# Decay products in 64-row tiles and skip coefficients per chunk of tokens, in a two-layer hybrid encoder

## What is computed

```python
def ssd_scan(xdt, a, bm, cm):
    ...
    a_cum = jnp.cumsum(a, axis=-1)
    lmat = jnp.exp(segsum(a))                 # exp(a_cum[i] - a_cum[j]) for i >= j, else 0
    cb = jnp.einsum("bclgn,bcsgn->bcgls", Cc, Bc)
    y_diag = jnp.einsum("bcgls,bgecls,bcsgep->bclgep", cb, lmat, X)
    ...
    y_off = jnp.einsum("bclgn,bcgepn,bgecl->bclgep", Cc, states_in, jnp.exp(a_cum))
    return (y_diag + y_off).reshape(b, s, h, p)
...
    y_f = ssd_scan(X * dt[:, :, 0, :, None], dt[:, :, 0] * A[0], bm, cm)
    flip = lambda t: jnp.flip(t, axis=1)
    y_b = flip(ssd_scan(flip(X * dt[:, :, 1, :, None]), flip(dt[:, :, 1] * A[1]), flip(bm), flip(cm)))
    y = y_f + y_b + X * d_skip[:, None]
```

## Time and profile before

| | |
|---|---|
| median of 3 executions | 1734.44 us |
| lowest, highest | 1731.61, 1737.55 us |
| the profiled execution | 1734.82 us |
| its span | 1733.1 us |
| TensorE busy | 1676.0 us (97%) |
| VectorE, ScalarE, GpSimd busy | 692.6, 636.9, 658.0 us |
| mean DMA rate | 307 GB/s |

### The profile page before, as it was taken

How to read it: one execution, slowest core, us unless ns; L and a number is a source line. 1 busy time by engine, 2 the same in 40 slices (tenths; PEclk the granted TensorE clock), 3 DMA queues, 4 the chain that set the end, 5 groups by cost and what they waited for, 6 DMA issues and landing times.

```text
span 1733.1 us, 22654 instructions
## 1 busy us (share of the span) xinstructions
PE 1676.0 (97%) x8727; PEld 1043.4 (60%) x8727; DVE 692.6 (40%) x1367; ACT 636.9 (37%) x1327; POOL 658.0 (38%) x532
## 2 busy tenths in 40 slices
PE   8999999999999999898999999999999999999998
PEld 6889777787434444343378897777864434444343
DVE  6738875524112212121176388745241212222122
ACT  5565566754111111111156555667441111111111
POOL 7888777894000000000077987778930000000000
PEclk9999999999999999999999999999999999999999
DMA  7554313758999999999954452227689999999997
GB/s 277 213 193 156 149 59 134 286 229 327 386 411 426 427 428 428 427 428 426 412 219 162 179 202 104 106 107 300 235 329 395 422 428 427 428 428 427 427 425 297
DMA packets 54193, 531.72 MB, mean 307 GB/s; under 512 B 7464, under 2 KB 11784, under 8 KB 23600
## 3 DMA queue, kind: packets, MB, share of 16 engines
q1 hardware_dynamic: 54048, 530.17, 74.8%
q0 software_dynamic: 32, 0.02, 0.0%
HBM read 528.71 MB, written 2.42 MB: 306 GB/s over the span
## 4 chain that ended last, share of the span: by engine, by line
PE 77%; DMA 11%; SPq 6%; ACT 2%; DVE 2%; issue 1%; POOL 1%; DVEq 0%; ACTq 0%
PE PS L1344 18%; DMA view<-in_w_exp_down_dram 11%; PE PS L1372 9%; PE PS L928 9%; PE PS L930 9%; PE PS L929 9%; SPq L699 5%; PE PS L1034 3%; PE PS L1035 3%; PE PS L1036 3%; PE PS L1284 2%; PE PS L1129 2%; PE PS L1270 1%; PE PS L1074 1%; PE PS L916 1%
## 5 line engine op out<-in xcount | busy, mean ns | idle before, releaser
L2414 POOL TENSOR_TENSOR view<-view,view 128x512 fp32r<-128x512 f32 x448 | 576.6, 1309 | 550.9 <-ACT view L1504 540.0
L1344 PE MATMUL PS<-view,view 128*64 128x512 f32 x2044 | 456.3, 598 | 20.8 <-issue 20.0
L1504 ACT ACTIVATE view<-view 128x512 fp32r<-128x512 f32 x448 | 273.7, 629 | 153.9 <-PE PS L930 150.4
L1344 PEld LDWEIGHTS PS<-view,view 128*64 128x64 f32 x2044 | 152.4, 137 | 294.9 <-issue 291.5
L928 PE MATMUL PS<-view,view 128*128 128x512 f32 x704 | 286.9, 407 | 5.4 <-POOL view L2414 3.5
L930 PE MATMUL PS<-view,view 128*128 128x512 f32 x704 | 276.2, 392 | 0.0
L929 PE MATMUL PS<-view,view 128*128 128x512 f32 x704 | 276.1, 392 | 0.0
L1372 PE MATMUL PS<-view,stb 128*64 128x512 f32 x1024 | 230.4, 597 | 8.2 <-DMA view<-in_w_exp_down_dram 5.4
L2321 DVE SCALAR_TENSOR_TENSOR view<-PS,gcol,view 128x512 fp32r<-128x512 f32 x64 | 48.1, 751 | 446.6 <-ACT view L1808 446.5
L928 PEld LDWEIGHTS PS<-view,view 128*128 128x128 f32 x704 | 133.1, 189 | 33.6 <-issue 6.1
L1372 PEld LDWEIGHTS PS<-view,stb 128*64 128x64 f32 x1024 | 71.7, 136 | 131.9 <-issue 115.2
(11 more groups left out here) (260 smaller groups left out, 1875.9 us busy)
## 6 DMA issues: line engine op xcount, KB each, us to landing
view<-in_w_exp_up_dram SPq DMA_DIRECT2D x56, 2048.0 KB, 27.3
view<-in_w_exp_down_dram SPq DMA_DIRECT2D x56, 2048.0 KB, 29.2
view<-in_w_mix_dram SPq DMA_DIRECT2D x54, 2048.0 KB, 7.6
view<-in_w_exp_gate_dram SPq DMA_DIRECT2D x52, 2048.0 KB, 30.3
view<-in_w_exp_gate_dram SPq DMA_DIRECT2D x20, 512.0 KB, 30.7
view<-in_w_exp_down_dram SPq DMA_DIRECT2D x20, 512.0 KB, 13.5
view<-in_w_exp_gate_dram SPq DMA_DIRECT2D x8, 1024.0 KB, 6.6
view<-in_w_exp_up_dram SPq DMA_DIRECT2D x8, 1024.0 KB, 8.7
```

Of the source, the lines that this page charges most:

```text
L1344: ins = pe.matmul(bank(ph, name, j)[e * CAP:(e + 1) * CAP, :], xgT1[:, k, at + e * CAP:at + (e + 1) * CAP], rows, start=(k == 0), stop=(k ...
L1504: nc.scalar.activation(highs(chunk), weights(slot8, chunk), ACT.Copy).then_inc(*high_ready.up(ph))
L2414: g_.tensor_tensor(weights(low8, chunk), weights(slot8, chunk), highs(chunk), ALU.subtract).then_inc(*low_ready.up(ph))
```

## The change

Two edits. The rows of direction 1 in the tile `terms` go from 32 to 64, and the decay products read 33 rows at 0 and 33 at 64; the 18 rows behind the 15 of the terms hold the frame's zeros. ROWS goes from 47 to 97, and with it the frame and each read of a tile.

The skip coefficients of chunk 0 are made in step 0 and those of chunk 1 in step 2, each behind that step's mask product, with the addition of d_skip for each chunk by itself. `decays` counts three instead of two, and GpSimd waits for its chunk's coefficients at each of its products with them.

```diff
--- before.py
+++ after.py
@@ -81,7 +81,8 @@
 UNITS_SCAN = TT * SSM_GROUPS
 SPLIT, FOUR = 3, 4
 TERMS = SPLIT * FOUR + SPLIT
-ROWS = 32 + TERMS
+HALF_ROWS, USED = 64, 33
+ROWS = HALF_ROWS + USED
 TERM_WORDS = (P + FOUR * P) // 2
 TERM_RING = 3
 FEED = (("v1", FB, -1, 5), ("ga", FB + 1, 5, 10), ("gm", FB + 2, 10, ATT))
@@ -123,8 +124,8 @@
     for d in range(2):
         for part in range(SPLIT):
             for n in range(FOUR):
-                frame[32 * d + part * FOUR + n, P + n * P:P + (n + 1) * P] = one
-            frame[32 * d + SPLIT * FOUR + part, 0:P] = one
+                frame[HALF_ROWS * d + part * FOUR + n, P + n * P:P + (n + 1) * P] = one
+            frame[HALF_ROWS * d + SPLIT * FOUR + part, 0:P] = one
     return np.ascontiguousarray(frame).view(np.float32)


@@ -522,7 +523,7 @@
         terms_out = sig("terms_out", 4 * SPLIT * TT, 0, step=16)
         terms_in = [sig(f"terms_in{k}", len(range(k, ATT, TERM_RING)), 0, step=16) for k in range(TERM_RING)]
         chosen = sig("chosen", ATT, 0)
-        decays = sig("decays", 2, 0)
+        decays = sig("decays", 1 + TT, 0)
         nmx_ready = sig("nmx_ready", ATT, 0)
         p_ready = sig("p_ready", ATT, 0)
         at_ready = sig("at_ready", ATT, 0)
@@ -712,7 +713,7 @@
                         for part, d, c in product(range(SPLIT), range(2), range(TT)):
                             src = rows_out[kind][part * SSM_HEADS:(part + 1) * SSM_HEADS].rearrange(
                                 "h (c d l) -> h c d l", c=TT, d=2)[:, c, d, :]
-                            row = 32 * d + (SPLIT * FOUR + part if kind else part * FOUR)
+                            row = HALF_ROWS * d + (SPLIT * FOUR + part if kind else part * FOUR)
                             at = (c * (ATT // TT) * ROWS + row) * TERM_WORDS + (P // 2 if kind else 0)
                             to = [[TERM_WORDS * ROWS, ATT // TT], [P // 2 if kind else TERM_WORDS, FOUR], [1, P // 2]]
                             sp.dma_start(bass.AP(terms_dram.tensor, at, to), src).then_inc(*terms_out.up(ph))
@@ -1059,7 +1060,7 @@
                     else:
                         pe.wait_ge(*M_ready.at(ph, i))
                     for d in range(2):
-                        t_ = terms[i % TERM_RING][32 * d:32 * d + TERMS, :].bitcast(BF16)
+                        t_ = terms[i % TERM_RING][HALF_ROWS * d:HALF_ROWS * d + USED, :].bitcast(BF16)
                         ins = pe.matmul(PS[:, 4 + d, :], t_[:, 0:P], t_[:, P:], start=True, stop=True)
                     ins.then_inc(*fill(ph, "D", j, q))

@@ -2104,19 +2105,17 @@
                         v.tensor_tensor(M[:, 4 * q:4 * q + 4, :], PS[:, 5, :].rearrange("p (h l) -> p h l", h=4),
                                         cbt[:, j, :].unsqueeze(1).to_broadcast([P, 4, P]), ALU.mult
                                         ).then_inc(*M_ready.up(ph))
-                    if i == 0:
-
-                        dve.wait_ge(*out_of(ph, "cb", 1))
-                        for c_ in range(TT):
-                            link(v.tensor_tensor(M[:, 4:8, :], cbt[:, c_ * SSM_GROUPS:(c_ + 1) * SSM_GROUPS, :],
-                                                 ident[:, :].unsqueeze(1).to_broadcast([P, SSM_GROUPS, P]), ALU.mult))
-                            link(v.tensor_reduce(cb_diag[:, c_, :], M[:, 4:8, :], AX, ALU.add))
-                        for c_ in range(TT):
-                            link(v.tensor_tensor(coef[:, c_, :].rearrange("p (g e) -> p g e", g=SSM_GROUPS),
-                                                 dtv[:, c_, SSM_HEADS:].rearrange("p (g e) -> p g e", g=SSM_GROUPS),
-                                                 cb_diag[:, c_, :].unsqueeze(2).to_broadcast([P, SSM_GROUPS, GH]), ALU.mult))
-                        v.tensor_tensor(coef, coef, bc_d.unsqueeze(1).to_broadcast([P, TT, SSM_HEADS]), ALU.add
-                                        ).then_inc(*decays.up(ph))
+                    if i in (0, 2):
+
+                        c_ = i // 2
+                        dve.wait_ge(*out_of(ph, "cb", c_))
+                        link(v.tensor_tensor(M[:, 4:8, :], cbt[:, c_ * SSM_GROUPS:(c_ + 1) * SSM_GROUPS, :],
+                                             ident[:, :].unsqueeze(1).to_broadcast([P, SSM_GROUPS, P]), ALU.mult))
+                        link(v.tensor_reduce(cb_diag[:, c_, :], M[:, 4:8, :], AX, ALU.add))
+                        link(v.tensor_tensor(coef[:, c_, :].rearrange("p (g e) -> p g e", g=SSM_GROUPS),
+                                             dtv[:, c_, SSM_HEADS:].rearrange("p (g e) -> p g e", g=SSM_GROUPS),
+                                             cb_diag[:, c_, :].unsqueeze(2).to_broadcast([P, SSM_GROUPS, GH]), ALU.mult))
+                        v.tensor_tensor(coef[:, c_, :], coef[:, c_, :], bc_d, ALU.add).then_inc(*decays.up(ph))
                 for k in range(XT):
                     low_of(ymTh[:, k, :], ymTl[:, k, :], ("mT", k), KD + k + 1, vcol[:, GS + k:GS + k + 1])
                 dve.wait_ge(*sumsq.at(ph, 13))
@@ -2454,6 +2453,7 @@
                 def skipped(j):

                     g = j % SSM_GROUPS
+                    pool.wait_ge(*decays.at(ph, 2 + j // SSM_GROUPS))
                     if j:
                         pool.wait_ge(*yo_ready.at(ph, j))
                     g_.tensor_tensor(heads(XD[:, :]), heads(Xtok[:, j // SSM_GROUPS, g * COLS:(g + 1) * COLS]),
@@ -2469,7 +2469,6 @@
                         to_end(j + 1)
                     fed(2 * j)
                     if j == 0:
-                        pool.wait_ge(*decays.at(ph, 2))
                         skipped(0)
                     pool.wait_ge(*out_of(ph, "off", j))
                     pool.wait_ge(*xD_ready.at(ph, j + 1))
```

## The result

| | before | changed |
|---|---|---|
| median | 1734.79 us | 1738.72 us |
| lowest, highest of 17 | 1731.61, 1740.43 us | 1735.16, 1743.63 us |
| ratio, 95% interval | | 1.0023 (1.0012 to 1.0034) |
| profiled execution, its span | 1734.82, 1733.1 us | 1737.41, 1735.7 us |

The change makes the kernel 3.9 us slower, where I had forecast 1722.8 us, 12 us faster.

A forecast was written before the change was run, and what follows sets the result against it. TensorE was taken to bound the scan's steps and the weight stream the expert stage, scan time counting one to one. Coefficients 8.0 plus tiles 3.6 gave 11.6 us off the 1734.44 median: 1722.8 us, range 1718 to 1729.

The forecast's parts named there:

- Transfers: Frame and reads of terms: growth from 58.8 to 121 KB a read, 0.7 us at the frame's rate, costs 0 us.
- The third rival: Terms land late, at 18 us; TensorE stands 5 us at two places of each layer: 1742.8 us, chance 0.04.
- Coefficients, first step: First scan step: half the coefficient work removed, so step 2 starts 4.3 us earlier, 2.8 of hole and 1.5 of clock.
- Coefficients, third step: Scan step i = 2: four VectorE instructions added, 1.8 to 3.8 us; cost on TensorE 0 to 1.1, taken as 0.3.
- The cover of 2.3 us: Third step: VectorE's waits of 0.33 and 2.00 us before the decay product's copy, taken to hide the added instructions.
- Rival 2: Third step pays back the first's gain, 1.1 us plus 1.5 of clock in each layer: 1727.4 us, chance 0.12 (either form).
- Decay products in 64-row tiles: Scan steps: score loads may run under decay products of equal height, 0.12 us a step, 30 steps, 3.6 us gained.
- rival 1: The tiles bring nothing, since loads still don't run ahead or heights are no mode: 1726.4 us, chance 0.20.
- The sum: Whole kernel: 8.0 us from coefficients plus 3.6 from tiles, 11.6 us gained, giving 1722.8 us.

The follow-up runs named there:

- 112 rows: Changed kernel with ROWS 112 in place of 97, the 15 more rows unused: 1723.99 us against 1735.55 for the kernel before, ratio 0.9927.
- the coefficients alone: Changed kernel with the tiles put back to 15 rows at 0 and 32, ROWS 47: 1729.0 us, ratio 0.9955 against the kernel before.
- Step 6: Changed kernel with ROWS 112 and chunk 1's coefficients made in step 6, not 2: ratio 0.9930 against the kernel before; repeated, 1720.90 us, 0.9917.
- tiles alone and 112 rows: Kernel before with 33 rows at 0 and 64 and ROWS 112, coefficients as before: 1728.74 us, ratio 0.9969 against the kernel before.
- the tiles alone: Kernel before with 33 rows at 0 and 64 and ROWS 97, coefficients as before: 1745.5 us, ratio 1.0050 against the kernel before.

## Why the prediction was wrong, point by point

**Transfers: the step that failed.** I put the growth of a read from 58.8 to 121 KB at "0.7 us at the frame's rate" and the cost at 0; it was 2.6 us. The frame is one transfer of all 16 tiles, at the rate of many engines (940 KB in 10.4 us, and 1940 KB in 13.3 us in the changed kernel, where I had about 21). A read of 47 rows had a rate of its own in the trace of before, 25 GB/s at a share of 0.07 (266 to 276 us above), which I didn't look at, nor did I weigh the rule on row counts quoted above, by which 97 rows go through one engine. By it the reads went from 2.4 to 5.0 us each, the batch of five before was still on the engine when the block was issued, and the first read behind the block was over 14.6 us after the block's issue where it had been after 9.5. The product wants it after 11.2 us (253.7 to 264.9 us with 112 rows). The price, by the changed kernel against 112 rows: step 11 to 12 takes 7.83 us for 3.87 and step 12 to 13 10.28 for 5.60 in layer 0, 7.44 for 3.87 and 7.19 for 5.61 in layer 1: 4.0 + 4.7 + 3.6 + 1.6 = 13.8 us. In half of it nothing waits; it is the clock, granted 0.50 from 268.6 to 278.8 us in layer 0 and from 1135.5 to 1139.0 us in layer 1, after TensorE had stood for 3.9 and 3.5 us.

The third rival had the mechanism at a chance of 0.04, with three wrong sizes. It wanted 18 us to landing to cost anything much, since it gave the read 13 us of lead, from steps of 5.3 us; the lead of the read behind the block was 11.2. It had two late reads in each layer, and there was one. And it had no term for the clock, though the hole of the first step showed one.

**Coefficients, first step: right.** Forecast 4.3 us in each layer; step 2 comes 4.5 and 4.3 us sooner, and with the coefficients alone as much. The granted clock is 1.00 from 207 to 215 us, and GpSimd's sum was over (211.3 us) before VectorE took it up (212.0).

**Coefficients, third step: mis-sized.** Forecast 0.3, at most 1.1; measured 1.45 with the coefficients alone (step 3 to 4: 5.51 for 4.06) and 1.8 with both parts. The timeline of the changed kernel (step 2 and 3):

```profile
208.84 1.31 DVE L2065 SCALAR_TENSOR_TENSOR view<-view,small 128x256 f32<-128x256 f32 x1
...
213.18 1.08 DVE L2112 TENSOR_TENSOR view<-view,ident 128x512 f32<-128x512 f32 x1
...
215.48 0.97 DVE L2118 TENSOR_TENSOR view<-view,bc 128x32 f32<-128x32 f32 x1
```

```profile
216.87 1.03 DVE L2065 SCALAR_TENSOR_TENSOR view<-view,small 128x256 f32<-128x256 f32 x1
...
217.96 0.44 PE L1140 MATMUL PS<-ident,view 128*128 128x128 f32 x2 [0.59 <-DVE view L2065]
...
220.33 0.68 DVE L2105 TENSOR_TENSOR view<-PS,view 128x512 f32<-128x512 f32 x1
...
221.16 0.39 PE L1064 MATMUL PS<-view 33*128 33x512 bf16 x2 [0.92 <-DVE view L2105]
```

The cover of 2.3 us was that of a VectorE which had come to step 2 with time in hand, as the step before had been long. Once that is short, VectorE works without a pause worth naming from step 1 on: its L2065 takes 1.31 us in step 2 beside GpSimd's work, before the four are reached, L2112 1.08 for 0.69, L2118 0.97 for 0.19 and the next L2065 1.03 for 0.48. Then L1140 waits 0.59 us and L1064 0.92 us for it. The two edits of one part were not independent: the one ate the other's cover. The four took 3.2 us, within my 1.8 to 3.8; what failed was the cover. Step 6, where VectorE has its 2.0 us of waiting, bears this out: the same four cost 0.4 us there. That GpSimd's work stretches VectorE's is read from where they overlap; no run took it away. Rival 2 (1.1 us, and 1.5 of clock) came nearer than the forecast: its wait was longer, and its clock fell in one layer of the coefficients alone and in none of the changed kernel.

**Decay products in 64-row tiles: right in kind, under-sized.** Forecast 0.12 us a step, bounds 0 and 0.2; measured 0.17 to 0.20 in the steps that TensorE bounds (7.16 to 6.99, 5.80 to 5.61, 4.06 to 3.87), 2.5 us to step 15 in layer 0 with tiles alone and 112 rows (layer 1's gain is hidden behind the clock there). The loads of the scores, first before, then after:

```profile
237.00 0.09 PEld L1063 LDWEIGHTS PS<-view 15*128 15x128 bf16 x2
237.01 0.39 PE L1063 MATMUL PS<-view 15*128 15x512 bf16 x2
...
237.32 0.30 PEld L1074 LDWEIGHTS PS<-view,view 64*128 64x128 f32 x4 [0.23 <-issue]
```

```profile
232.23 0.10 PEld L1064 LDWEIGHTS PS<-view 33*128 33x128 bf16 x2
232.23 0.39 PE L1064 MATMUL PS<-view 33*128 33x512 bf16 x2
232.24 0.42 PEld L1075 LDWEIGHTS PS<-view,view 64*128 64x128 f32 x4
```

The loads start 10 ns behind the decay products instead of 0.31 us, and L1075's group takes 0.43 us where L1074's took 0.63; L1064's own 0.32 stays, as forecast. This fits a cost for each change of height, one of which is gone. The edit changed place and height together, and 15 rows at 64 were not tried. The rule on row groups, which spoke for rival 1, doesn't hold here: the pair of decay products reaches into all four groups, and the loads run under it, as L931's load (206.79 us in the changed kernel) runs under L930's product (206.78), both of 128 rows. So where the Trainium skill (TensorE: Matmul & The Clock Gate, The mechanism) lets a load overlap only with other row groups, the measurement decides; the same section also lets a load go ahead into a background weight buffer, and that fits. The Trainium skill (TensorEngine Tiling (Array Packing), Key Properties) on the drain at a change of mode fits as well.

**The sum.** With 112 rows the same two edits give 4.96 and 4.80 us in the steps, and 1723.99 us where I had 1722.8. That this is so near is luck: in 8.0 + 3.6 the gain was put too high by what the third step costs (1.8 us for 0.3 in each layer), and too low a little in the first step and by more in the tiles. The changed kernel's profile adds up from there: 9.8 gained less 13.8 lost is 4.0 us slower in the steps; the table has 3.7 + 0.4.

## What to carry to other kernels

When an edit grows a transfer, look for the rate of that very transfer, in a stretch where it runs alone, before any rate of another; a DMA share of 0.07, with two packets at once, looks like one engine of 16. Keep row counts of DMAs to numbers that split over the engines: 97 rows took 5.0 us, 98 about one. And a wait that is shortened takes away the slack that the next step had from it, so price an addition there in the new schedule, not in the old one.

## What the runs showed of the hardware

- A read from DRAM of 47 or 97 rows of 1280 bytes ran at 24 to 25 GB/s alone, with a DMA share of 0.07 and never more than two packets at once; reads of 48, 98 and 112 rows at a median of 131, 157 and 174 GB/s, with 9 to 21 packets at once. One unused row more, 98 for 97, took a read from 5.0 to 0.8 us.
- Waits of TensorE of 3.5 to 3.9 us cost 4.7 us more in one layer and 1.6 in the other (3.2 and 4.5 with the tiles alone), by how long the clock stayed at its lower level, 1.2 GHz: 10.2 and 3.5 us. Behind the same hole of 2.8 us it stayed there 3.5 us in the kernel before and 10.3 us in one layer with the tiles alone and 112 rows, where steps 1 to 3 took 3.7 us longer than in the other layer.
- Weight loads of 64 rows, at 0 and at 64, started 10 ns behind decay products of 33 rows at the same two places; where the products had 15 rows at 0 and at 32, they started 0.31 us behind them.
